# Router of a top-4 mixture of experts: an fp32 gather of the unnormalised x, with a selection matrix that carries 1/rms, in place of a three-part bf16 split of the normalised x

## What is computed

```python
x = x + mixed @ w_out[l]
x = x + moe_ffn(rms_norm(x, g_ffn[l]), w_router[l], b_router[l], w_e1[l], b_e1[l], w_e2[l], b_e2[l])

def moe_ffn(h, ...):
    logits = hf @ w_router + b_router
    top_v, top_i = lax.top_k(logits, TOP_K)          # 4 of 32
    gates = jax.nn.softmax(top_v, axis=-1)
    # for every expert e, over the tokens that chose it:
    u = xb @ w_e1[e] + b_e1[e]                       # 1024 -> 2048
    act = clamp(u_even) * sigmoid(1.702 * clamp(u_even)) * (clamp(u_odd) + 1)
    y = act @ w_e2[e] + b_e2[e]                      # 1024 -> 1024, weighted by the gate, added to x
```

## Time and profile before

| what | us |
|---|---|
| median of 3 runs | 1237.48 |
| the three runs | 1231.65, 1237.48, 1239.58 |
| the profiled execution's own time | 1239.21 |
| its span (first to last instruction) | 1237.4 |
| PE busy in the span | 1136.9 (92%) |
| share of the chain that ended last: DMA of expert weights / PE | 44% / 42% |

### The profile page before, as it was taken

How to read it: one execution, slowest core, us unless ns; L and a number is a source line. 1 busy time by engine, 2 the same in 40 slices (tenths; PEclk the granted TensorE clock), 3 DMA queues, 4 the chain that set the end, 5 groups by cost and what they waited for, 6 DMA issues and landing times.

```text
span 1237.4 us, 17251 instructions
## 1 busy us (share of the span) xinstructions
PE 1136.9 (92%) x7218; PEld 564.4 (46%) x7218; DVE 375.1 (30%) x620; ACT 267.7 (22%) x405; POOL 123.4 (10%) x42
## 2 busy tenths in 40 slices
PE   6979999998999999999889889999999999999986
PEld 5978789986433333333333333333333333333332
DVE  6786663694411121111111111122111111111112
ACT  5446564423111111111111111111111111111112
POOL 6332462432000000000000000000000000000000
PEclk9989999999999999999999999999999999999999
DMA  7533323948999999999999999999999999999995
GB/s 297 196 136 123 129 107 120 365 158 323 367 386 427 431 426 427 428 426 430 428 428 429 427 429 427 431 426 430 430 427 430 427 431 426 430 430 427 429 427 215
DMA packets 35825, 448.13 MB, mean 362 GB/s; under 512 B 4160, under 2 KB 4288, under 8 KB 6576
## 3 DMA queue, kind: packets, MB, share of 16 engines
q1 hardware_dynamic: 34992, 445.99, 86.5%
q0 software_dynamic: 368, 1.24, 0.3%
q10 hardware_dynamic: 432, 0.42, 0.1%
HBM read 446.58 MB, written 1.05 MB: 362 GB/s over the span
## 4 chain that ended last, share of the span: by engine, by line
DMA 44%; PE 42%; DVE 8%; issue 2%; ACT 2%; POOL 1%; SPq 0%; DVEq 0%; ACTq 0%
DMA ring<-wexp 44%; PE PS L817 23%; PE PS L557 9%; PE PS L810 3%; PE PS L802 2%; PE PS L874 1%; ACT slot_R L918 1%; DVE slot_R L1149 1%; PE PS L653 1%; DVE EXT L1187 1%; DVE slot_R L1169 1%; PE PS L869 0%; DVE EXT L1218 0%; DVE BRW L1185 0%; DVE BE L1186 0%
## 5 line engine op out<-in xcount | busy, mean ns | idle before, releaser
L817 PE MATMUL PS<-ring,SQ 128*64 128x512 f32 x2016 | 455.0, 596 | 61.7 <-DMA ring<-wexp 61.4
L817 PEld LDWEIGHTS PS<-ring,SQ 128*64 128x64 f32 x2016 | 138.3, 136 | 352.9 <-issue 227.3
L817 PE MATMUL PS<-ring,PTG 128*64 128x512 f32 x1024 | 226.8, 595 | 0.0
L817 PEld LDWEIGHTS PS<-ring,PTG 128*64 128x64 f32 x1024 | 70.7, 137 | 152.2 <-issue 133.2
L1562 DVE TENSOR_SCALAR SQ<-PS 128x512 f32<-128x512 f32 x32 | 22.1, 692 | 364.9 <-PE PS L817 364.9
L1096 ACT ACTIVATE SQ<-SQ 128x512 f32<-128x512 f32 x32 | 20.2, 630 | 500.6 <-DVE SQ L1562 500.6
L487 POOL TENSOR_TENSOR slot_R<-ring,slot_R 128x2048 fp32r<-128x2048 f32 (+1 forms) x20 | 98.3, 4916 | 148.4 <-ACT slot_R L918 148.3
L1553 DVE TENSOR_TENSOR PTG<-TAB,GR 128x128 bf16<-128x128 f32 x32 | 9.4, 292 | 333.8 <-PE PS L862 333.8
L557 PE MATMUL PS<-slot_R 128*128 128x256 f32 (+1 forms) x296 | 95.4, 322 | 0.0
L918 ACT ACTIVATE slot_R<-ring 128x2048 fp32r<-128x2048 f32 (+1 forms) x38 | 71.8, 1890 | 44.0 <-PE PS L557 21.9
L557 PE MATMUL PS<-HT_R,slot_R 128*128 128x256 f32 x400 | 76.4, 293 | 4.9 <-ACT ring L956 2.8
(11 more groups left out here) (264 smaller groups left out, 977.0 us busy)
## 6 DMA issues: line engine op xcount, KB each, us to landing
ring<-wexp SPq DMA_DIRECT2D x190, 2048.0 KB, 33.4
ring<-wblk SPq DMA_DIRECT2D x36, 1024.0 KB, 4.9
EXT<-wexp SPq DMA_DIRECT2D x2, 2048.0 KB, 9.1
BRW<-brow SPq DMA_DIRECT2D x7, 256.0 KB, 5.0
ring<-wskv SPq DMA_DIRECT2D x2, 768.0 KB, 11.3
EXT<-x SPq DMA_DIRECT2D x2, 512.0 KB, 4.5
out<-EXT SPq DMA_DIRECT2D x3, 256.0 KB, 2.0
EXT<-gfin POOLq DMA_DIRECT2D x1, 512.0 KB, 9.4
```

What stands on the lines that cost most here:

```text
L817: last = mm(PS[g * SLOTS:(g + 1) * SLOTS, b, :], lhsT, rhs[:, g * 512:(g + 1) * 512], start=start, stop=stop)
```

## The change

1. x gets a buffer of its own (X); SQR takes x's former place in EXT1, so that EXT1 is free once the mixing is over.
2. `norm` and the three-part split are gone: two normalisations, seven roundings and subtractions on DVE, ACT and POOL, and their semaphores.
3. The gather multiplies X itself, fp32, by an fp32 SEL: 16 fp32 matmuls instead of 48 bf16 ones.
4. SEL gets one more DVE step, a product with the token's 1/rms: at the first expert and in the loop.
5. The mask is bf16 and so are the triangular matrix and the ones (TRIB, made by POOL in the dense part); the five ranking matmuls are bf16.
6. DVE compares the indices as they are (uint32) with the experts' numbers, in two halves; the conversion is gone, and the negated maxima move behind the mask.
7. PE computes all four residual products before it waits for the mask.
8. SP issues chunk 8 into EXT1 ahead of chunk 7, behind `mix_lo`; chunk 9 goes into EXT0 behind `lg_full` alone. PE takes chunk 8 from EXT1 and chunk 9 from EXT0.
9. g_final is loaded into the upper half of GR when the output projection has been read, instead of behind the tenth used chunk.

```diff
             for c in range(EARLY, NCHUNK):
+                if c == NCHUNK - 1:
+                    sp.wait_ge(mix_lo, 4)
+                    sp.dma_start(EXT1[:], wexp[NCHUNK]).then_inc(ext_in[0], 16)
                 first_chunk(c)
             sp.wait_ge(lg_full, 1)
-            sp.wait_ge(xp1, 2)
-            sp.wait_ge(rest1, 1)
-            sp.wait_ge(rp1, 1)
-            sp.dma_start(EXT0[:], wexp[NCHUNK]).then_inc(ext_in[0], 16)
-            sp.wait_ge(resid_done, 1)
-            sp.wait_ge(ssq1, 2 * TT)
-            sp.dma_start(EXT1[:], wexp[NCHUNK + 1]).then_inc(ext_in[1], 16)
+            sp.dma_start(EXT0[:], wexp[NCHUNK + 1]).then_inc(ext_in[1], 16)
...
-            pool.wait_ge(xp1, 1)
-            nc.gpsimd.tensor_tensor(REST[:, 1, :], xn[:, 1, :], XP[0][:, 1, :], ALU.subtract).then_inc(rp1, 1)
-            pool.wait_ge(xp2, 1)
-            nc.gpsimd.tensor_tensor(XP[2][:, 1, :], REST[:, 1, :], XP[1][:, 1, :], ALU.subtract).then_inc(rp2, 1)
...
             def gather():
                 for k in range(KT):
-                    for n in range(3 * TT):
-                        last = mm(PS[:, 7, k * SLOTS:(k + 1) * SLOTS], XP[n // TT][:, n % TT, k * P:(k + 1) * P],
-                                  SEL[:, n % TT, :], start=(n == 0), stop=(n == 3 * TT - 1))
+                    for i in range(TT):
+                        last = mm(PS[:, 7, k * SLOTS:(k + 1) * SLOTS], X[:, i, k * P:(k + 1) * P], SEL[:, i, :],
+                                  start=(i == 0), stop=(i == TT - 1))
...
-            for n, i in enumerate((1, 0)):
-                act.wait_ge(xn_ready, n + 1)
-                fn(XP[0][:, i, :], xn[:, i, :], ACT.Copy).then_inc(xp1, 1)
-            act.wait_ge(rp1, 1)
-            fn(XP[1][:, 1, :], REST[:, 1, :], ACT.Copy).then_inc(xp2, 1)
-            act.wait_ge(rest1, 1)
-            fn(XP[1][:, 0, :], REST[:, 0, :], ACT.Copy).then_inc(xp2, 1)
...
-                    v.tensor_tensor(SEL, iota, spread(RK[:, :, bass.ds(done + 1, 1)]), ALU.is_equal).then_inc(sel_ready, 1)
+                    v.tensor_tensor(SEL, iota, spread(RK[:, :, bass.ds(done + 1, 1)]), ALU.is_equal).then_inc(sel_raw, 1)
                     v.tensor_tensor(SELG, iota2, spread2(RK[:, :, bass.ds(done, 1)]), ALU.is_equal).then_inc(selg_raw, 1)
                     v.tensor_copy(SELE, hot(bass.ds(T_HOT + (e + 1) % NE, 1))).then_inc(sele_ready, 1)
+                    dve.wait_ge(sel_raw, done + 1)
+                    v.tensor_tensor(SEL, SEL, scales, ALU.mult).then_inc(sel_ready, 1)
```

More of the change, by code:

```diff
@@ L149, in program @@
         SQ = sb("SQ", shapes["SQ"])
-        SQR = sb("SQR", shapes["SQR"])
         EXT1 = sb("EXT1", [P, CHW])
-        X = EXT1[:, 0:SLOTW].rearrange("p (i d) -> p i d", i=TT)
+        SQR = EXT1[:, 0:SLOTW].rearrange("p (i d) -> p i d", i=TT)
+        X = sb("X", [P, TT, D])
+        TRIB = sb("TRIB", [P, 2, P], BF16)
         SIG = EXT1[:, SLOTW:SLOTW + D]
@@ L197, in program @@
         S_V8 = [small(98 + 8 * i, 8) for i in range(TT)]
-        S_IF = [small(114 + 8 * i, 8) for i in range(TT)]
         S_NV = [small(130 + i, 1) for i in range(TT)]
@@ L225, in program @@
         HTf = HT[:].rearrange("p k t -> p (k t)")
-        xn = GV
         xnT = HT
@@ L254, in program @@
         SELG = PTf[:, 1024:1280].rearrange("p (i r c) -> p i r c", i=TT, r=2)
-        SEL = PTf[:, 1280:1344].bitcast(BF16).rearrange("p (i c) -> p i c", i=TT)
-        SELE = PTf[0:3 * NE, 1344:1376].bitcast(BF16)
+        SEL = PTf[:, 1280:1408].rearrange("p (i c) -> p i c", i=TT)
+        SELE = PTf[0:3 * NE, 1408:1440].bitcast(BF16)
         KDf = KD[:].rearrange("p i d -> p (i d)")
@@ L306, in program @@
         ext_in = [sem(f"ext_in{n}") for n in range(EXTRA)]
-        resid_done, cnt_read = sem("resid_done"), sem("cnt_read")
+        cnt_read = sem("cnt_read")
         chunk_used = sem("chunk_used")
@@ L490, in _ @@
                     pool.wait_ge(row_in, 16)
+                    pool.wait_ge(tab_in, 16)
+                    nc.gpsimd.tensor_copy(TRIB[:, 0, :], TAB[:, T_TRI:T_TRI + P]).then_inc(tri_ready, 1)
+                    nc.gpsimd.memset(TRIB[:, 1, :], 1.0).then_inc(tri_ready, 1)
                 if u in (19, 20):
@@ L786, in _ @@
             residual(1, 0)
-            tri, ones = TAB[:, T_TRI:T_TRI + P], TAB[:, T_ONE:T_ONE + P]
+            residual(0, 1)
+            residual(1, 1)
+            tri, ones = TRIB[:, 0, :], TRIB[:, 1, :]
+            pe.wait_ge(tri_ready, 2)
             pe.wait_ge(mask_ready, 1)
@@ L839, in chunk @@
                         pe.wait_ge(ext_in[n - NCHUNK], 16)
-                        data = (EXT0, EXT1)[n - NCHUNK][:]
+                        data = (EXT1, EXT0)[n - NCHUNK][:]
                     else:
@@ L1476, in _ @@
                                               ROW[:, R_ROUTER:R_ROUTER + NE], ALU.mult, ALU.add)
-            last.then_inc(lg_read, 1)
-            norm(0)
-            dve.wait_ge(lg_read, 1)
+            link(last)
             for i in range(TT):
@@ L1483, in _ @@
             for i in range(TT):
-                v.tensor_scalar(S_NV[i], S_V8[i][:, 0:1], -1.0, None, ALU.mult).then_inc(top_ready, 1)
                 last = v.max_index(IDX[i][:], S_V8[i], LG[:, i, :])
             link(last)
+            top = [P, TT, TOPK, NE]
+            experts = TAB[:, T_IOTA:T_IOTA + NE].unsqueeze(1).broadcast_to([P, TOPK, NE])
             for i in range(TT):
-                last = v.tensor_copy(S_IF[i], IDX[i][:])
+                last = v.tensor_tensor(OH[:, i], experts, IDX[i][:, 0:TOPK].unsqueeze(2).broadcast_to([P, TOPK, NE]),
+                                       ALU.is_equal)
             link(last)
-            top = [P, TT, TOPK, NE]
-            experts = TAB[:, T_IOTA:T_IOTA + NE].unsqueeze(1).unsqueeze(1).broadcast_to(top)
-            indices = SM[:, 114:114 + 8 * TT].rearrange("p (i k) -> p i k", i=TT)[:, :, 0:TOPK]
-            link(v.tensor_tensor(OH, experts, indices.unsqueeze(3).broadcast_to(top), ALU.is_equal))
-            v.tensor_reduce(MK, OH.rearrange("p i k e -> p i e k"), AX_X, ALU.add).then_inc(mask_ready, 1)
-            dve.wait_ge(xp1, 2)
-            v.tensor_tensor(REST[:, 0, :], xn[:, 0, :], XP[0][:, 0, :], ALU.subtract).then_inc(rest1, 1)
+            v.tensor_reduce(MK, OH.rearrange("p i k e -> p i e k"), AX_X, ALU.max).then_inc(mask_ready, 1)
+            for i in range(TT):
+                v.tensor_scalar(S_NV[i], S_V8[i][:, 0:1], -1.0, None, ALU.mult).then_inc(top_ready, 1)
             dve.wait_ge(mask_ready, 1)
@@ L1512, in hot @@
                 return TAB[0:3 * NE, a].broadcast_to([3 * NE, SLOTS])
-            v.tensor_tensor(SEL, iota, spread(RK[:, :, 0:1]), ALU.is_equal).then_inc(sel_ready, 1)
+            scales = spread(S_RS.unsqueeze(2))
+            link(v.tensor_tensor(SEL, iota, spread(RK[:, :, 0:1]), ALU.is_equal))
+            v.tensor_tensor(SEL, SEL, scales, ALU.mult).then_inc(sel_ready, 1)
             v.tensor_copy(SELE, hot(slice(T_HOT, T_HOT + 1))).then_inc(sele_ready, 1)
-            dve.wait_ge(xp2, 2)
-            v.tensor_tensor(XP[2][:, 0, :], REST[:, 0, :], XP[1][:, 0, :], ALU.subtract).then_inc(xp3, 1)
             v.memset(RK[:, :, PASSES * NE:PASSES * NE + 1], 1e6)
```

37 lines of the change are left out of this document (13 added, 24 removed).

## The result

| | before | after |
|---|---|---|
| median, us (20 runs each) | 1238.47 | 1242.73 |
| lowest to highest | 1230.04 to 1239.98 | 1235.23 to 1246.41 |
| the profiled execution's own time / span | 1239.21 / 1237.4 | 1244.30 / 1242.0 |

The ratio is 1.0038, with a 95% interval of 1.0021 to 1.0054: 4.3 us slower, less than 1%. The sum had +1.3 us. Between the two profiled executions the difference is +4.6 us of span, and that is what is taken apart here.

The account below looks back on a forecast made before the run. The DMA weight stream was taken as the bound. Chunk 18's issue -0.7 (start -4.1, two gathers +3.4), landing +0.3 and last gather +1.7 gave +1.3 on 1237.48, so 1238.8 us; range 1231 to 1246.

Parts of the forecast that it names:

- The sum: Whole kernel: start, gathers before chunk 18, its landing and the last gather together add 1.3 us, giving span 1238.7, median 1238.8.
- rival 2: First gather and ranking: PE's clock falls to half, gather takes 6.92 us, +3.8, time 1242.6; chance 0.13.
- only four of 33 gathers are on the path: The first gather, two before chunk 18 and the last count; with gather time g the change is 4g - 12.6.
- the start: From the read of the logits to the first chunk's matmuls: 4.1 us sooner, first chunk at 312.9.
- only about 1 us without work is left ahead of the gather: PE ahead of the first gather: residual products fill the wait, so the clock was expected to stay high.
- Mask and ranking sum: Behind the logits: mask ready at 307.2 to 307.3, 2.0 us earlier; five bf16 ranking matmuls 0.4, DVE's L1499 under 0.29.
- no delay: Three residual products behind the logits' end, 0.80 us each, fill PE from 304.8 to 307.2 without holding up the mask's path.
- the gather: Each expert's gather as 16 fp32 matmuls: 3.46 us against 1.51, of which 1.71 per expert shows.
- the landing of chunk 18: DMA of chunk 18 into an empty queue: 7.9 us against 7.4, between 0 and +0.5, taken as +0.3.
- Rival 1: Gather: weight loads hide and only moving columns count, 1.71 us, time 1231.9; chance 0.12.
- Rival 3: Whole expert loop: PE becomes the bound, ending at 1097.4 + 33g against DMA's 1224.8 + 4g, crossing at g = 4.39; chance 0.06.
- 27 us inside: End of the kernel: PE by itself would end at 1211.6, 27 us ahead of the DMA-set end.

Follow-up runs that it names:

- old_all: Changed kernel with every gather back at 48 bf16 matmuls, reading TRIB so the experts get other inputs; 1231.95 us, 0.9947 of the kernel before.
- old_loop: Changed kernel with 48 bf16 matmuls on TRIB only in the gathers of experts 4 to 31; 1241.83 us, 1.0034 of the kernel before.
- ring: Changed kernel with chunks 18 and 19 loaded into EXT1 and EXT0 again, so chunk 18 waits for PE's ninth use; 1237.41 us, 1.0000 of the kernel before.
- fill: Changed kernel plus one unneeded fp32 128x512 product on PE behind the ranking, filling its wait for SEL; 1241.6 us, 1.0036 of the kernel before.
- after_b: Changed kernel run again unedited, on one chip with a repeat of the kernel with the filling product; 1244.15 us, 1.0047 of the kernel before.
- stat: Changed kernel with the gather turned round: SEL stationary, X moving in rows of 512, ACT copy and four transposes; 1235.4 us, 0.9982 of the kernel before.
- twice: Changed kernel with every gather done twice, the second writing the same result again; one run, 1337.76 us, span 1335.9.
- all3: Changed kernel with the turned gather, the product filling PE's wait, and chunks 18 and 19 into EXT1 and EXT0 again; 1229.86 us, 0.9935 of the kernel before.

## Why the forecast was right in class and off in size

**Right: no gain, a small loss.** The time lies in the range and within 1%, and its sign is that of the sum. The size isn't: +4.3 where the sum had +1.3. That the median of 1242.73 stands next to rival 2's 1242.6 is luck in part: the cold start cost 2.9 and not 3.8, dearer gathers and a later landing made up for it, and 1.0 us comes from the kernel before, whose median over 20 runs is 1238.47 and not 1237.48. What carried the forecast is that only four of 33 gathers are on the path, which `old_all` and `old_loop` show, and that removed work and dearer gathers nearly cancel.

**Wrong: the start (-4.1, measured -0.7).** The failed step is "only about 1 us without work is left ahead of the gather", from which I took that the clock would stay high. PE did wait about 1 us (306.49 to 307.51), and the clock fell all the same, at 309.95, when PE had been on the first gather for 2.4 us. A wait of 1 us with this gather behind it was followed by a fall in five profiles of six; why not in `ring` stays open. Rival 2 came true in this trace, and its price was mis-sized. I had put 3.8 on it, the whole gather at half clock and 0.3 of ranking; the ranking ran at 1.00, only the second half of the gather was slow (4.89 and not 6.92), but the first chunk behind it was too (5.42 instead of 3.65), which I had left out. Together 2.9, by `fill`. The Trainium skill, "TensorE: Matmul & The Clock Gate", section "Part 1: The HAM clock gate", describes a clock that is throttled by default and released by the activity of the array, and gives the two levels of 1.2 and 2.4 GHz. The trace agrees on the levels; that the clock would fall while the gather was running, and with a wait of only 1.0 us ahead of it, I had not drawn from it.

The rest of the miss at the start, 0.5, stands in `fill`, whose clock held: the gather began 3.81 behind LG (forecast 3.6) and took 3.80 (3.46).

**Confirmed at the start, but for one term.** Mask and ranking sum, from DVE's timeline of the kernel after:

```profile
305.46 0.59 DVE L1466 TENSOR_REDUCE GR<-GR 128x64 bf16<-128x256 f32 x1
...
306.09 0.19 DVE L1470 TENSOR_SCALAR GR<-GR 128x64 f32<-128x64 bf16 x1
306.58 0.22 DVE L1472 TENSOR_TENSOR GR<-GR,PS 128x64 f32<-128x64 f32 x1 [0.30 <-PE PS L787]
```

L1470 is L1499 of the earlier trace rows: 0.19 us with POOL idle, where it was 2.12 beside POOL's L503. The mask stood 2.35 behind LG (306.05), against 2.2 to 2.3 forecast from its own LG. L783 to L787 took 0.24 and not 0.4. The term that had "no delay" is the residual products: they took 2.66 for three and not 2.4, ended at 306.25, and so held the ranking for 0.2 us behind the mask, which is most of what the gather began too late.

**Mis-sized: the gather (3.46, measured 3.71).** The earlier trace rows gave 1.73 for 16 records, and I doubled it. In both kernels the records start 0.112 us apart; the first of the 16 in the earlier trace rows started only 0.055 ahead of the next, since the loads ran beside the end of the work ahead (0.055 + 15 x 0.112 = 1.73). In the new gather the first two take 0.159 and 0.113. A group of 16 is thus no half of a group of 32. Each gather is 2.00 on the path and not 1.71 (48.58 - 44.57 is twice that), and 2.0 in the tail: 3.71 - 1.51, less 0.20 that the transposes behind it take less. This is 0.9 of the 3.3 us of error.

**Mis-sized: the landing of chunk 18 (+0.3, measured +0.9).** The issue moved to an empty queue as forecast, but there the landing took 8.3 and not 7.9. It was 7.7 in `fill` with the same gap, and 7.9 in `after_b`, the same kernel again: the scatter is that large, and I have no cause for it.

**Rival 1 is refuted**: 3.71, and 0.112 us per record with a load of 192 ns each, at 64 moving columns. `stat` shows from the other side that the loads count: with four times fewer of them, the same product takes 1.72. **Rival 3** did not happen at g = 3.71. Its line for PE, 1097.4 + 33g, gives 1338.0 for `twice` (g = 7.29), and the span was 1335.9. So close is luck: from LG on the line gives 1033.0 and the run took 1040.5, of which I put 6.1 down to its cold start (21.99 from LG to chunk 10, against 12.29 + 3.58 by `fill` and the longer gather), while its dense part was 9.6 us shorter. Against 1224.8 + 4g for the stream it leaves 20 us of room at 3.71.

**What the forecast left out.** It counted PE as "27 us inside" at the end, and it had the first DMA of weights in the chain near the fifteenth expert instead of the eighth; measured it starts at 771.25, in the seventeenth, instead of 525.25, in the eighth. What it didn't draw from this is that PE, with a lead of 1.4 us per expert over the stream, can't make use of an earlier chunk 18: a fix of the hole ahead of chunk 18 pays in full only with a faster gather (`ring` 3.3 us, `all3` against `stat` 5.6).

## What to carry to other kernels

Where a stream of weights sets the end, count only the instances of an operation that lie ahead of the point from which the queue stays filled, and behind the last landing; here 4 of 33. A conversion that exists only to make a multiplication cheap should be compared with turning the product around: here, with both operands fp32, the one with few columns was the better stationary one (2.30 us with its transposes, against 3.71). And a saved microsecond can buy less than it says if it leaves TensorE with a wait ahead of small matmuls: read the granted clock of that stretch, and price the low clock over all that stands behind the wait, not over the first group alone.

## What the hardware did that I had not expected

- The clock fell 2.4 us into a busy gather, after a wait of 1.0 us, and stayed at 0.50 for 6.8 us, though PE was busy throughout; with the doubled gather of `twice` it stayed there for 13.7 us. It held in both profiles with a 128x512 product in that wait, and in `ring` without one. In `old_all` and `stat` it held without the filler, with a wait as long (303.99 to 305.02, and 298.53 to 299.55) and a bf16 or a turned gather behind it. Whether the form of the product behind the wait decides it, or only the moment at which it comes, these runs don't separate.
- An fp32 product of a 128x128 stationary and 64 moving columns runs at 0.112 us per record, two records each, in groups of 16 records as of 32. The 32-column router product (L762, 16 records) has the same spacing, so half the columns bring nothing.
- Turned around, the same multiplications take 8 records in 1.72 us, pairs of which start 7 ns apart and then 423 ns: two products into the two halves of the partitions ran side by side.
- The landing of chunk 18 (2 MB), issued to an empty or nearly empty queue, took 7.4 us in the kernel before and 7.6 to 8.3 in the nine other profiles with the old ring, while streamed chunks followed each other every 4.90.
